# First loads of a two-layer hybrid decoder trunk: x repacked in two halves on one queue, the identity built on GpSimd, and the first block's matmuls by fours

## What is computed

```
def rms_norm(x, g):
    y = x * lax.rsqrt(jnp.mean(x * x, axis=-1, keepdims=True) + EPS)
    return y * g

def swiglu(x, w_gate, w_up, w_down):
    return (jax.nn.silu(x @ w_gate) * (x @ w_up)) @ w_down

for l in range(DEPTH):                                   # DEPTH = 2
    x = x + 0.5 * swiglu(rms_norm(x, ffn1_norm[l]), ffn1_w_gate[l], ffn1_w_up[l], ffn1_w_down[l])
    h = rms_norm(x, mix_norm[l]); proj = h @ w_in[l]
    ...
    x = x + merged @ w_out[l]
    x = x + 0.5 * swiglu(rms_norm(x, ffn2_norm[l]), ffn2_w_gate[l], ffn2_w_up[l], ffn2_w_down[l])
```

## Time and profile before

| what | value |
| --- | --- |
| median of 3 runs | 1044.41 us (1044.19 to 1044.72) |
| the profiled execution's own time | 1044.15 us |
| its span | 1042.4 us |
| TensorE busy | 1037.6 us (100% of the span, rounded) |
| VectorE, ScalarE, GpSimd busy | 718.0, 585.8, 62.8 us |
| granted TensorE clock | 0.9 or more of full in all 40 slices |
| HBM read | 186.04 MB |

### The profile page before, as it was taken

One profiled execution on the slowest core, in us unless ns is written; L12 is line 12 of the kernel. 1 busy time (PEld: TensorE's weight loads), 2 busy tenths in 40 slices (PEclk: granted clock), 3 DMA queues, 4 the chain that ended last, 5 costly groups with the idle time before them and its releaser, 6 DMA issues.

```text
span 1042.4 us, 15577 instructions
## 1 busy us (share of the span) xinstructions
PE 1037.6 (100%) x5656; PEld 897.7 (86%) x5656; DVE 718.0 (69%) x1132; ACT 585.8 (56%) x935; POOL 62.8 (6%) x69
## 2 busy tenths in 40 slices
PE   9999999999999999999999999999999999999998
PEld 8888888998888888888888888889988888888887
DVE  6766666668786876666686666666688868676665
ACT  6555455466963754554565455455678646454552
POOL 1052000112100000000000000001211000000000
PEclk9999999999999999999999999999999999999999
DMA  7765544455435455555545555634454346545541
GB/s 265 247 222 188 207 163 166 138 182 190 150 122 202 168 189 192 206 186 204 180 147 202 201 187 182 213 130 151 160 202 162 122 162 222 202 162 200 191 172 61
DMA packets 35269, 187.60 MB, mean 180 GB/s; under 512 B 4496, under 2 KB 4640, under 8 KB 20128
## 3 DMA queue, kind: packets, MB, share of 16 engines
q1 hardware_dynamic: 34704, 186.03, 51.0%
q0 software_dynamic: 240, 0.53, 0.2%
q10 hardware_dynamic: 288, 0.54, 0.2%
HBM read 186.04 MB, written 1.05 MB: 179 GB/s over the span
## 4 chain that ended last, share of the span: by engine, by line
PE 99%; DVE 0%; issue 0%; ACT 0%; DVEq 0%; ACTq 0%
PE ps L1364 96%; PE ps L1784 1%; PE ps L1388 1%; PE ps L1375 1%; PE ps L1811 1%; PE ps L1847 0%; PE ps L1694 0%; DVE hT L1000 0%; PE ps L1686 0%; PE ps L1412 0%; DVE x L993 0%; ACT hT L602 0%; DVE w_lo L911 0%; PE ps L1400 0%; DVE kTA L863 0%
## 5 line engine op out<-in xcount | busy, mean ns | idle before, releaser
L1364 PE MATMUL ps<-hT,w_hi 128*128 128x512 f32 x1408 | 341.5, 391 | 0.2 <-DVE hT L1000 0.2
L1364 PEld LDWEIGHTS ps<-hT,w_hi 128*128 128x128 f32 x1408 | 259.0, 188 | 50.3 <-DVE hT L1000 0.5
L878 DVE TENSOR_TENSOR w_lo<-w_raw,w_hi 128x2048 fp32r<-128x2048 f32 x82 | 188.0, 2293 | 87.3 <-ACT w_hi L541 87.3
L1364 PEld LDWEIGHTS ps<-hT,w_lo 128*128 128x128 f32 x1408 | 180.9, 191 | 7.4
L1364 PE MATMUL ps<-hT,w_lo 128*128 128x256 f32 x1408 | 182.9, 283 | 0.0
L1364 PE MATMUL ps<-w_hi,hT 128*128 128x512 f32 (+2 forms) x576 | 174.6, 377 | 0.0
L541 ACT ACTIVATE w_hi<-w_raw 128x2048 fp32r<-128x2048 f32 x85 | 161.9, 1905 | 13.4 <-PE ps L1364 13.2
L1364 PE MATMUL ps<-w_lo,aTh 128*128 128x512 f32 x352 | 137.1, 389 | 0.0
L1364 PE MATMUL ps<-w_hi,aTl 128*128 128x512 f32 x352 | 137.0, 389 | 0.0
L1364 PE MATMUL ps<-w_hi,aTh 128*128 128x512 f32 x352 | 136.8, 390 | 0.0
L570 ACT ACTIVATE S<-ps 128x256 f32<-128x256 f32 x88 | 33.7, 383 | 159.3 <-PE ps L1364 159.3
(11 more groups left out here) (166 smaller groups left out, 958.8 us busy)
## 6 DMA issues: line engine op xcount, KB each, us to landing
w_raw<-in_w_ffn SPq DMA_DIRECT2D x85, 1024.0 KB, 4.9
w_raw<-in_w_ffn SPq DMA_DIRECT2D x92, 512.0 KB, 5.6
w_raw<-in_w_gate SPq DMA_DIRECT2D x16, 1024.0 KB, 4.9
w_raw<-in_w_proj SPq DMA_DIRECT2D x16, 592.0 KB, 4.8
w_raw<-in_w_branch SPq DMA_DIRECT2D x8, 1024.0 KB, 4.7
w_raw<-in_w_out SPq DMA_DIRECT2D x8, 1024.0 KB, 4.8
w_raw<-in_w_uq SPq DMA_DIRECT2D x4, 384.0 KB, 2.9
SG<-in_w_ffn SPq DMA_DIRECT2D x1, 1024.0 KB, 10.6
```

What stands on the lines that cost most here:

```text
L878: dve.tensor_tensor(wl_gu[b], raw_gu[b], wh_gu[b].bitcast(F32), ALU.subtract).then_inc(lo_gu.sem, 1)
L1364: return pe.matmul(dst, w, m, start=start, stop=stop, skip_group_check=True)
```

## The change

1. The host packs x in two blocks: `x_first`, per partition 32 columns of norm gains (31 used) and the first 512 columns of both token tiles (1056 columns, 528 KB), and `x_second`, the other 512 columns of both (512 KB). In SBUF they lie one behind the other in `x_cols`, ahead of them nothing changes but the addresses; x is now indexed half, token tile, column. Both are loaded by SyncE's queue, and ScalarE's queue issues nothing at the start.
2. The identity is no longer loaded. GpSimd makes it with a memset and an `affine_select`; `masks_in` loses its first plane.
3. Block 0's weights come in four loads of 256 KB, each with its own semaphore, instead of two of 512 KB.
4. `small_in`, the signal that the gains are there, is raised by GpSimd once `x_first` has landed.
5. ScalarE and VectorE take four chunks of x first, then quarter 0, chunks 4 and 5, quarter 1, chunks 6 and 7, quarters 2 and 3.
6. TensorE: `keep_warm(7)`, the transposes of chunks 0 to 3 after `x_first`, one more warm product, the transposes of chunks 4 to 7 after `x_second`, and then block 0 as four high and four low matmuls at a time.

The diff, cut to its core (the uses of x in its new layout are left out but for one):

```diff
+        x_cols = sb("x_cols", [P, COLS_PAD + TT * D_MODEL])
+        x = x_cols[:, COLS_PAD:].rearrange("p (h t n) -> p h t n", h=2, t=TT)
+        cols = x_cols[:, 0:7 + 3 * KC]
...
         def _(sp):
-            x_tokens = x_in.rearrange("b (t p) d -> p (b t) d", p=P)
-            sp.dma_start(x[:, 0, :], x_tokens[:, 0, :]).then_inc(x_in_done[0].sem, 16)
-            sp.dma_start(ident[:, :], masks_in[0, :, 0:P]).then_inc(ident_in.sem, 16)
-            for s in range(2):
-                part = slice(s * KC * P, (s + 1) * KC * P)
-                sp.dma_start(raw_gu[0][:, part], w_ffn[0, :, part]).then_inc(start_in[s].sem, 16)
-            for s, sem in enumerate((start_in[2].sem, raw_gu_in[1].sem)):
+            part = slice(0, COLS_PAD + TT * HALF)
+            sp.dma_start(x_cols[:, part], x_first_in).then_inc(x_in_done[0].sem, 16)
+            sp.dma_start(x_cols[:, COLS_PAD + TT * HALF:], x_second_in).then_inc(x_in_done[1].sem, 16)
+            for i in range(4):
+                sp.dma_start(raw_gu[0][:, start_cols(i)], w_ffn[0, :, start_cols(i)]).then_inc(start_in[i].sem, 16)
+            for s, sem in enumerate((start_in[4].sem, raw_gu_in[1].sem)):
...
             pool.memset(minus_half[:, :], -0.5).then_inc(half_set.sem, 1)
+            pool.memset(ident[:, :], 0.0).then_inc(ident_set.sem, 1)
+            pool.wait_ge(ident_set.sem, 1)
+            pool.affine_select(ident[:, :], ident[:, :], [[1, P]], ALU.not_equal, 1.0, base=0, channel_multiplier=-1)\
+                .then_inc(ident_set.sem, 1)
             pool.wait_ge(half_set.sem, 1)
 
-            for t in range(TT):
-                pool.wait_ge(x_in_done[t].sem, 16)
+            pool.wait_ge(x_in_done[0].sem, 16)
+            pool.sem_inc(small_in.sem, 16)
+            pool.wait_ge(x_in_done[1].sem, 16)
             pool.sem_inc(x_done.sem, 2 * TT)
...
         def _(act):
-            act.dma_start(x[:, 1, :], x_in.rearrange("b (t p) d -> p (b t) d", p=P)[:, 1, :]).then_inc(x_in_done[1].sem, 16)
-            act.dma_start(cols[:, :], cols_in[0]).then_inc(small_in.sem, 16)
-
...
-                    act.wait_ge(start_in[i % 2].sem, 16)
+                    act.wait_ge(start_in[i].sem, 16)
...
-                    columns_high(0, range(0, 2))
+                    columns_high(0, range(0, 4))
                     start_high(0)
-                    columns_high(0, range(2, 4))
+                    columns_high(0, range(4, 6))
                     start_high(1)
-                    columns_high(0, range(4, 6))
+                    columns_high(0, range(6, 8))
                     start_high(2)
-                    columns_high(0, range(6, 8))
                     start_high(3)
...
-            dve.wait_ge(ident_in.sem, 16)
...
-                        part = x[:, t, h * HALF:(h + 1) * HALF]
+                        part = x[:, h, t, :]
...
             pe.wait_ge(warm_set.sem, 1)
-            keep_warm(12)
-            pe.wait_ge(ident_in.sem, 16)
+            keep_warm(7)
+            pe.wait_ge(ident_set.sem, 2)
...
+                    pe.wait_ge(x_in_done[0].sem, 16)
+                    for c in range(4):
+                        column_start(c)
+                    keep_warm(1)
+                    pe.wait_ge(x_in_done[1].sem, 16)
+                    for c in range(4, KC):
+                        column_start(c)
+                    start_high_four(0, 0)
+                    start_low_four(0, 0)
+                    start_high_four(1, 0)
+                    start_low_four(1, 0)
+                    start_high_four(0, 1)
+                    start_low_four(0, 1)
+                    start_high_four(1, 1)
+                    start_low_four(1, 1)
```

More of the change, by code:

```diff
@@ L62 @@
 RS_BANK = 5
+COLS_PAD = 32
 PROJ_GROUPS = ((0, 384), (384, 768), (768, PROJ_COLS))
@@ L218, in build @@
         x_in_done = [signal(f"x_in_done{h}", 0) for h in range(2)]
-        start_in = [signal(f"start_in{i}", 0) for i in range(3)]
+        start_in = [signal(f"start_in{i}", 0) for i in range(5)]
         third_in = signal("third_in", 0)
@@ L414, in _ @@
                 sp.wait_ge(x_done.sem, x_done.at(DEPTH - 1, 4 * TT + i))
-                sp.dma_start(out[0, t * P:(t + 1) * P, half], x[:, t, half]).then_inc(out_done.sem, 16)
+                sp.dma_start(out[0, t * P:(t + 1) * P, half], x[:, i // 2, t, :]).then_inc(out_done.sem, 16)
             sp.wait_ge(out_done.sem, 16 * 2 * TT)
@@ L1070, in _ @@
                 if l == 0:
[L1071 removed]
+                    columns_low(0, range(0, 4))
                     start_low(0)
[L1073 removed]
+                    columns_low(0, range(4, 6))
                     start_low(1)
[L1075 removed]
+                    columns_low(0, range(6, 8))
                     start_low(2)
[L1077 removed]
                     start_low(3)
@@ L1387, in transposed, with column_start @@
                         for t in range(TT):
-                            ins = pe.transpose(dst[:, t * P:(t + 1) * P], x[:, t, c * P:(c + 1) * P], ident[:, :])
+                            ins = pe.transpose(dst[:, t * P:(t + 1) * P], x[:, c // 4, t, c % 4 * P:(c % 4 + 1) * P], ident[:, :])
                         ins.then_inc(ht_ps.sem, 1)
-                def columns_start():
+                def column_start(c):
+                    if c >= 6:
+                        pe.wait_ge(ht_lo.sem, ht_lo.at(0, c - 6))
+                    dst = x_place(0, 0, c)
                     for t in range(TT):
[L1394 to L1401, removed]
+                        ins = pe.transpose(dst[:, t * P:(t + 1) * P], x[:, c // 4, t, c % 4 * P:(c % 4 + 1) * P], ident[:, :])
+                    ins.then_inc(ht_ps.sem, 1)
                 def columns(layer, n, h):
@@ L1495, in gate_up_first @@
                     spread_rs(w)
-                def gate_up_start():
[L1499 to L1519, removed]
@@ new lines, in start_high_four @@
+                def start_high_four(s, half):
+                    if 2 * half + s < 3:
+                        pe.wait_ge(start_hi.sem, 2 * half + s + 1)
+                    else:
+                        pe.wait_ge(hi_gu.sem, hi_gu.at(0, 0))
+                    for k in range(4 * half, 4 * half + 4):
+                        if s == 0:
+                            pe.wait_ge(ht_lo.sem, ht_lo.at(0, k))
+                        c = (s * KC + k) * P
+                        high(s, wh_gu[0][:, c:c + P], k, k == 0)
@@ new lines, in start_low_four @@
+                def start_low_four(s, half):
+                    if 2 * half + s < 3:
+                        pe.wait_ge(start_lo.sem, 2 * half + s + 1)
+                    else:
+                        pe.wait_ge(lo_gu.sem, lo_gu.at(0, 0))
+                    for k in range(4 * half, 4 * half + 4):
+                        c = (s * KC + k) * P
+                        ins = low(s, wl_gu[0][:, c:c + P], k, k == KC - 1)
+                    if half == 1:
+                        ins.then_inc((gate_ps, gu_used)[s].sem, 1)
```

39 lines of the change are left out of this document (19 added, 20 removed).

## The result

| what | before | after |
| --- | --- | --- |
| median | 1044.3 us (1044.09 to 1044.72, 4 runs) | 1057.44 us (1056.85 to 1057.92, 4 runs) |
| ratio, 95% interval | | 1.0126 [1.0114, 1.0139] |
| the profiled execution's own time, span | 1044.15, 1042.4 | 1056.85, 1055.1 |

The change costs 13.1 us. The forecast was 3.7 us, and the range ended at 1051.3: the sign was right by luck, for a reason that turned out wrong, and the size is far outside.

A forecast was written before the change was run, and what follows sets the result against it. It took TensorE as the bound, busy 1037.6 of 1042.4 us. To 1044.15 it added 2.1 for the late identity, net of fours, and 1.5 for the clock: 1047.75, plus 0.26 to the median, 1048.0 us; range 1042.4 to 1051.3.

The forecast's parts named there:

- The new layout of x changes addresses alone.: x in SBUF: the repacking into two halves was taken to cost no time.
- the edits at nothing: Edits given no effect on time: ScalarE's dropped issues, `small_in` over GpSimd, SyncE's extra loads, the x layout, the reciprocal root.
- The price of the configuration, +2.1 us: GpSimd's pool configuration ahead of the select: 6.2 us, making the identity late; block 0 ends 2.1 us later, net of fours.
- The clock, +1.5 us: TensorE's start: pausing from 4.2 to 8.4 us might drop its clock to the lower level; 1.5 us taken, bound 5.6.
- The first rival: GpSimd's configuration costs nothing, identity in time: block 0 ends 1.8 us earlier, 1042.6 us in total; chance 0.34.
- T: When TensorE loads its first transpose: 6.12 us before, 8.4 forecast, 4.5 if the identity is in time.
- One sentence on the bytes: SyncE's queue at the start: eleven loads instead of nine, with the same bytes less 80 KB.
- The fours, 0.2 us: Block 0 by four chunks instead of pairs: it ends at T + 8.4 instead of T + 8.58, gaining 0.2 us.
- the case that I had worked out: Block 0 by fours, with TensorE never waiting for the later quarters of the weights.
- a little before ScalarE asks: Block 0's 256 KB weight quarters land 0.6 us apart, from 6.3 to 8.3, each before ScalarE needs it.

The follow-up runs named there:

- e1: The kernel before with an unused tile of 128 bytes per partition between x and `hT`, no instruction changed: 1058.49 us.
- e11: e9 with the identity loaded behind `x_second` instead of made on GpSimd: median 1045.08 us, ratio 1.0006 to the kernel before.
- e2: The changed kernel with an unused tile behind `x_cols`, filling the two up to 12288 bytes per partition: 1042.57 us.
- e9: The changed kernel with 128 unused bytes behind `x_cols`, 8448 bytes together: median 1043.25 us, ratio 0.999 to the kernel before.
- e4: The changed kernel with `keep_warm(11)` instead of `keep_warm(7)`: 1057.96 us.
- e8: The kernel before with 128 unused bytes behind `hT`, ahead of `aTh`: 1051.49 us.
- e10: e9 with ScalarE, VectorE and TensorE working block 0 in pairs as before: median 1043.83 us, ratio 0.9997 to the kernel before.

## Why the prediction was wrong

**"The new layout of x changes addresses alone."** This is the step that failed, and it stood among the edits at nothing. It was true as a statement of what changes, and its price was 14.5 us (e1, which has that part alone), four times the whole forecast. I had read the sizes of the tiles only for what their loads take, and had worked out a matmul's time from its columns alone. The Trainium skill (SBUF — State Buffer, Operand start alignment) asks for a start at a multiple of the element size and says that its runs timed nothing. The runs here time it: a start 128 bytes further, well inside that rule, costs 14.5 us.

**The price of the configuration, +2.1 us, was the wrong end of its bound.** I had bounded it by 0 and 9.8 and taken 6.2, from the landing times of GpSimd's own DMAs, which were the nearest rows in kind only if code is fetched at all. The whole pause in which it stands is 0.26 us, and the select starts within 0.1 us of it. The row that bore on it directly, the arithmetic at 15.79 that follows its releaser without a delay, was named for the rival and outweighed. The Trainium skill (GPSIMD Engine Reference, 2.1 Instruction dispatch) has about 6 us for the first call into freshly loaded code; the select here, behind the same instruction, starts within 0.1 us of it, so the trace shows no such price for this operation. Whether code was there already or none is needed, no run tells.

**The clock, +1.5 us:** it rested on a reading that does not hold. I took the clock as full from the start and asked what a pause would take away. The pace of the warm products (0.22 us each, against 0.11 for the transposes after 6.20) shows TensorE at half its pace for the first 6 us of the kernel before, so the question was when the clock rises. In the changed kernel it rose at 5.00, ahead of block 0, and cost it nothing there. A pause of 4 us, as I had forecast, did not occur; e11's pause of 1.92 us, with the rise at 10.01, cost about 1 us.

**The first rival was right for the opening.** It said T = 4.5 and block 0's end at 12.9. T was the start of the first weight load; that is 4.56 in the changed kernel and 4.43 in e2, and block 0 ends at 13.16 and 13.09. e2's 1042.57 us meets the rival's 1042.6, but the median of eleven runs of e9 is 0.65 above it. x_first landed at 4.46 (said: 4.4), and ScalarE waited 1.07 us, until 15.02, for `third_raw` (said: there at 14.8) and TensorE not at all, as argued. Block 0 begins at T + 2.90 (said: 2.8) and takes 5.70 (said: 5.58). The 128 bytes are not the reason for the longer block: e2 and e9, with their matmuls at 391 ns, take 5.71. Its first four high matmuls take 1.02 us and the later fours 0.92 to 0.94. One sentence on the bytes was wrong: SyncE's queue carries 464 KB more than before (1040 of x and gains, against 512 of x and 64 of the identity), and both queues together 64 KB less, not 80; the landings hardly showed it.

**The fours, 0.2 us:** in the case that I had worked out they gain almost nothing: block 0 ends at T + 8.60 in the changed kernel against T + 8.58 before, and, where all transposes ran at the full pace, 8.37 us behind the first transpose in e4 (fours) against 8.42 in e8 (pairs). Where the weights come late they gained 0.6 to 0.7 (e9 against e10), which is another case.

**What I missed at the start** is that a quarter's landing is not one number. I had the first quarter at 6.3, "a little before ScalarE asks". It landed 5.0 us after its issue at 1.65 in the changed kernel, 4.9 in e2, just in time for ScalarE at 6.76 and 6.69, and 6.04 us after it, at 7.7, in e9's profiled run.

**Left open.** Why the distance matters is not shown: the runs tell that it is the distance between the weight tiles and the tile that a product reads beside them, and that 256 bytes more is as 0, and no row shows what inside TensorE or SBUF they share. TensorE loads weights while it streams (PEld is busy 85% of the span and PE 100%), and the next matmul's weights have the same distance here, so it is not shown either which of the two loads meets the stream. Nor is it shown why 192 bytes slow the high matmuls and speed up the low ones. That it repeats beyond 256 bytes rests on e2 alone (4096 bytes more). What makes the first quarter of the weights land late in some runs, and when the clock rises, no run was made to tell. Distances under 64 bytes, and a distance chosen for each kind of product by itself (192 for the low ones, 0 for the high), were not tried; the latter could beat e9.

## What to carry to other kernels

A tile that is resized or added moves every tile behind it, so it is an edit to all matmuls that read those tiles. Where TensorE is the bound, compare the start-to-start time of one untouched group of long matmuls before and after any such edit, before looking at anything else, and pad the tile so that the distance between stationary and moving operands keeps its remainder by 256 bytes. These kernels bear that out; others were not tried. When a total moves by far more than the edited stretch holds, look first for a small change in each instance of a large group: 5 ns on some 3,000 matmuls is 15 us. And judge the clock at a kernel's start by the pace of equal instructions, not by the clock row alone.

## What the hardware did that I had not expected

- A matmul of 512 columns in this kernel, with its weight load beside it, takes 226 ns from start to start where the distance between its operands is as in the kernel before or 256 bytes more, and 232.5 ns where it is 128 bytes more (the table above). The pace of the transposes, and so the clock, is the same.
- The loss is there with ScalarE and VectorE idle as well (226.7 ns before, 234.2 with 128 bytes more).
- The low matmuls of 256 columns go the other way: 1.82 us for sixteen at 192 bytes, 1.92 at 0.
- The pool configuration ahead of a select of 128x128 stands in a pause of 0.26 us; memset and select take 0.20 and 0.28 us.
- The first 256 KB of weights behind 1040 KB on one queue land 4.9 and 5.0 us after their issue in two runs (e2 and the changed kernel) and 6.0 in two others (e9 and e10).
- TensorE works at half its pace until 5.00 us in the changed kernel, 6.20 in the kernel before and 10.01 in e11, while the clock row of each page shows 9s.
